# One phase for the output projection and the MLP, with the second norm's factor applied after w_up

## The chip, the core and the metric

The kernel runs on one core of one Trainium2 chip. The metric is the device time of one execution in microseconds (us). The core's engines run side by side and meet only at semaphores: PE multiplies matrices (its weight loads are shown as PEld), ACT and DVE work element by element and can read the matmul banks, POOL works element by element on on-chip memory, and SP issues the DMAs.

## What is computed

One layer of a hybrid decoder, for 1,040 prompt tokens (16 of them learned meta tokens) and 8 sequences of 4 sampled tokens. The part that matters here is what follows the attention and the convolution:

```python
mix = jnp.concatenate([_rmsnorm(attn, attn_out_g), _rmsnorm(conv, conv_out_g)], axis=-1)
x = x + mix @ w_o                          # 1024 x 1024
hf = _rmsnorm(x, norm_ffn_g)               # x * rsqrt(mean(x*x) + EPS) * gain
return x + jnp.square(jax.nn.relu(hf @ w_up)) @ w_down      # 1024 x 4096, 4096 x 1024
```

## The kernel before

Six phases follow one another: `inputs`, `prompt_attention`, `sample_attention`, `output_projection`, `mlp` and `store_outputs`. Each ends with a barrier of all engines (L321). Activations are kept transposed: features on the 128 partitions, 1,074 columns of tokens in 3 blocks of 358 (`NBLK`, `TB`), so that the residual stream `xT` has 8 chunks of 128 features (`KD`).

Weight products come close to float32 by splitting: a number is kept as a rounded part `hi` and a remainder `lo`, and each product takes three matmul passes, hi by hi, hi by lo and lo by hi. A weight tile of 128 output columns goes through a `Ring` of two slots: SP loads `raw`, ACT rounds it to `hi` (`split_hi`, L229), POOL subtracts (`split_lo`, L233). `split_hi` waits until the slot's last product is done (`used`), SP's next load until `split_lo` is done (`lo_done`). `Ring.products` (L236, matmuls at L244) then issues for each chunk k the three passes over three blocks, 72 matmuls for a `KD`-chunk tile, into three banks of slot 0 or of slot 1, and waits before that until those banks have been emptied (`evacuated`).

`Norm` (L97) is an RMS norm over features. ACT and DVE square the chunks, POOL adds pairs, PE sums over partitions by matmuls with ones (L152), DVE takes the mean (L158), ACT the root (L165), DVE the reciprocal (L161), PE spreads the factor over the partitions (L171) and ACT copies it out of the banks (L176). Only then does DVE scale chunk by chunk (L181), ACT round `hi` (L191), and DVE and POOL in turn subtract `lo` (L196, L201).

`output_projection` (L1808) runs two such norms over 4 chunks each, then 8 tiles of `w_o`. The first two are issued interleaved as the normed chunks come (`paired_products`, L249, matmuls at L266), the other six in a loop; after each, DVE adds the banks into its chunk of `xT` (L1894). After the barrier `mlp` (L1897) starts with the norm over all 8 chunks of `xT` and pairs the first two `w_up` tiles. It then works in 8 groups of 4 tiles of `w_up` (f = 0 to 3) and 8 tiles of `w_down` (m = 0 to 7, 4 chunks each). After a `w_up` product ACT applies the relu from the banks (L1949) and squares into `a_hi` (L1953), DVE squares again (L2035) and subtracts (`a_lo`, L2038). The first `w_down` product takes chunk k only when `a_lo` of f = k is done (`act_ready`). DVE adds each `w_down` product into `xT` (L2045).

## Time and profile before

| | us |
|---|---|
| three runs | 2112.9, 2110.64, 2107.7; median 2110.64 |
| the profiled execution, whole | 2108.73 |
| its span, first to last instruction | 2107.0 |
| PE busy in the span | 2002.8 (95%) |
| DVE, ACT, POOL busy | 928.2, 796.6, 428.4 |

In the span the output projection begins at 1179 us, the MLP at 1302 us and the store of the outputs at 2088 us. All starts below are counted from the span's first instruction. "Granted clock" (PEclk) is the share of full TensorE speed that the chip allowed: 1.00 is 2.4 GHz, 0.50 is 1.2 GHz, and a value between the two is a mean over a stretch with both. A row's idle time stands in square brackets or behind a bar, with what ended it.

### The profile page before, as it was taken

How to read it: one execution, taken by the hardware profiler on the slowest of the kernel's cores; microseconds unless marked ns; L12 is line 12 of the kernel's file. 1: busy time of each engine (PE TensorE's matmuls, PEld its weight loads, DVE VectorE, ACT ScalarE, POOL GpSimd, SP SyncE). 2: the span in 40 equal slices, each digit the busy share in tenths (PEclk: the TensorE clock that was granted, in tenths of full speed). 3: DMA queues.
4: the chain of work that ended last, by engine and by line, in shares of the span. 5: the costliest groups of instructions: out<-in, count | busy, mean ns of one | idle time of the engine just before them, and what ended most of it. 6: DMA issues, size and time to landing. Idle time of an engine off the chain costs nothing. (4 is left out here: it accounts for less than half of the span.)

```text
span 2107.0 us, 38039 instructions
## 1 busy us (share of the span) xinstructions
PE 2002.8 (95%) x13358; PEld 1877.5 (89%) x13358; DVE 928.2 (44%) x1679; ACT 796.6 (38%) x1702; POOL 428.4 (20%) x391
## 2 busy tenths in 40 slices
PE   6999997999969999999999698899999999999998
PEld 5999985777749999999998496799999999999998
DVE  6125145556536777777777622521222222221222
ACT  5012134656635666666666311311121111212121
POOL 3233133111010000010000323331222222231221
PEclk7999998999979999999999598899999999999999
DMA  6122000000022222222222111020202011120202
GB/s 213 50 64 63 10 19 9 1 1 0 0 71 63 77 74 73 70 75 73 74 69 107 40 40 29 22 61 26 75 15 65 25 55 50 30 61 24 75 15 97
DMA packets 180599, 108.42 MB, mean 51 GB/s; under 512 B 52132, under 2 KB 177154, under 8 KB 180276
## 3 DMA queue, kind: packets, MB, share of 16 engines
q1 hardware_dynamic: 180358, 107.21, 17.7%
q8 instruction: 44, 0.72, 0.1%
q10 hardware_dynamic: 174, 0.30, 0.1%
q14 instruction: 23, 0.19, 0.0%
HBM read 97.47 MB, written 10.00 MB: 51 GB/s over the span
## 5 line engine op out<-in xcount | busy, mean ns | idle before, releaser
L1750 PE MATMUL banks<-comb_hi,pageT_hi 128*128 128x272 f32 x1024 | 234.3, 310 | 0.0
L1640 DVE TENSOR_REDUCE k_sums<-k_sq 128x8 f32<-128x512 f32 x256 | 174.4, 681 | 92.3 <-ACT k_sq L1462 92.3
L1750 PE MATMUL banks<-comb_hi,pageT_lo 128*128 128x272 f32 x1024 | 212.5, 289 | 0.0
L1750 PE MATMUL banks<-comb_lo,pageT_hi 128*128 128x272 f32 x1024 | 212.2, 289 | 0.0
L1462 ACT ACTIVATE k_sq<-banks 128x512 f32<-128x512 f32 x256 | 152.0, 594 | 142.4 <-PE banks L1750 139.4
L2045 DVE TENSOR_TENSOR xT<-xT,banks 128x1074 f32<-128x1074 f32 x64 | 81.5, 1274 | 277.4 <-PE banks L244 277.4
L2035 DVE TENSOR_TENSOR relu_squared<-relu 128x1074 f32<-128x1074 f32 x32 | 40.9, 1278 | 305.2 <-ACT relu L1949 305.2
L1949 ACT ACTIVATE relu<-banks 128x1074 f32<-128x1074 f32 x32 | 34.3, 1071 | 360.3 <-PE banks L244 351.9
L244 PE MATMUL banks<-a_hi,w_down_hi 128*128 128x358 f32 x768 | 168.2, 327 | 0.0
L244 PE MATMUL banks<-a_hi,w_down_lo 128*128 128x358 f32 x768 | 167.7, 326 | 0.0
L244 PE MATMUL banks<-a_lo,w_down_hi 128*128 128x358 f32 x768 | 167.6, 326 | 0.0
L233 POOL TENSOR_TENSOR w_down_lo<-w_down_raw,w_down_hi 128x512 fp32r<-128x512 f32 x64 | 94.7, 1479 | 348.0 <-ACT w_down_hi L229 348.0
L1750 PEld LDWEIGHTS banks<-comb_lo,pageT_hi 128*128 128x128 f32 x1024 | 161.8, 189 | 0.0
L1750 PEld LDWEIGHTS banks<-comb_hi,pageT_lo 128*128 128x128 f32 x1024 | 161.0, 190 | 0.0
L1750 PEld LDWEIGHTS banks<-comb_hi,pageT_hi 128*128 128x128 f32 x1024 | 158.1, 191 | 0.0
L244 PE MATMUL banks<-hf_hi,w_up_lo 128*128 128x358 f32 x720 | 157.5, 327 | 0.0
L244 PE MATMUL banks<-hf_hi,w_up_hi 128*128 128x358 f32 x720 | 157.0, 326 | 0.3 <-POOL w_up_lo L233 0.3
L244 PE MATMUL banks<-hf_lo,w_up_hi 128*128 128x358 f32 x720 | 157.1, 326 | 0.0
L244 PEld LDWEIGHTS banks<-a_hi,w_down_hi 128*128 128x128 f32 x768 | 133.3, 189 | 0.0
L244 PEld LDWEIGHTS banks<-a_hi,w_down_lo 128*128 128x128 f32 x768 | 132.8, 189 | 0.0
L244 PEld LDWEIGHTS banks<-a_lo,w_down_hi 128*128 128x128 f32 x768 | 131.6, 189 | 0.0
L229 ACT CAST w_down_hi<-w_down_raw 128x512 fp32r<-128x512 f32 x64 | 39.5, 617 | 237.4 <-PE banks L244 237.4
(371 smaller groups left out, 4044.3 us busy)
## 6 DMA issues: line engine op xcount, KB each, us to landing
page_latents<-in_cache_kv_latent SPq DMA_DIRECT2D x256, 128.0 KB, 2.1
w_up_raw<-in_w_up SPq DMA_DIRECT2D x32, 512.0 KB, 4.2
w_down_raw<-in_w_down SPq DMA_DIRECT2D x64, 256.0 KB, 2.8
w_in_raw<-in_w_in SPq DMA_DIRECT2D x17, 512.0 KB, 3.8
x_spill<-xT SPq DMA_DIRECT2D x1, 4296.0 KB, 13.9
xT<-x_spill SPq DMA_DIRECT2D x1, 4296.0 KB, 12.8
page_ropes<-in_cache_k_rope SPq DMA_DIRECT2D x256, 16.0 KB, 1.8
w_o_raw<-in_w_o SPq DMA_DIRECT2D x8, 512.0 KB, 4.2
```

Source lines behind the costliest of these rows:

```text
L229: act.copy(self.hi[s][:, :, :], self.raw[s][:, :, :]).then_inc(self.hi_done[s], 1)
L233: nc.gpsimd.tensor_sub(self.lo[s][:, :, :], self.raw[s][:, :, :], self.hi[s][:, :, :].bitcast(F32)).then_inc(self.lo_done[s], 1)
L244: mm = pe.matmul(out[:, b, 0:TB], w[s][:, k, :], x(k)[:, b * TB:(b + 1) * TB], start=k == 0 and a == 0, stop=k == self.K - 1 and a == 2)
L1462: act.activation(sq[j % 2][:, :].rearrange("p (a c) -> p a c", a=2), kn[:, :, 0:WK], ACT.Square)\
L1640: nc.vector.tensor_reduce(ksum[par][:, j, :], sq[j % 2][:, :].rearrange("p (h c) -> p h c", h=H), AX_X, ALU.add)\
L1750: mm = pe.matmul(banks[:, 2 * (j % 2) + half, 0:WC], x[j % AHEAD][:, k, :], w[par][:, k, half, :], start=k == 0 and a == 0, stop=k == KL - ...
L1949: act.activation(relu[:, f % 2, :].rearrange("p (b t) -> p b t", b=NBLK), banks[:, 3 * (f % 2):3 * (f % 2) + 3, 0:TB], ACT.Relu)\
L2035: nc.vector.tensor_mul(full[:, s, :], relu[:, s, :], relu[:, s, :]).then_inc(sq_done, 1)
L2045: nc.vector.tensor_add(x, x, banks[:, 3 * s:3 * s + 3, 0:TB]).then_inc(down.evacuated[s], 1)
```

## The change

The two phases become one, `output_and_mlp`, and the norm before the MLP is taken apart in a new class `LateNorm`. Its per-token factor is a positive number, so it can be taken out of `hf @ w_up` and through the relu: the products are made from `x * gain`, and the factor is multiplied in when the results of `w_up` leave the banks.

- `w_o` and `w_up` share one ring and its two slots of banks; SP loads `w_up` tiles behind the `w_o` tiles. The loop over `w_o` tiles 2 to 7 is written out on every engine. `w_down` keeps its ring, now in memory that held the convolution's and the attention's results, so its first loads wait for the last `w_o` product.
- As soon as DVE has added tile m into `xT`, ACT rounds `x * gain` of that chunk and squares the chunk, DVE subtracts the remainder, POOL adds the square to a running total.
- PE sums the total over partitions inside the first `w_up` product (f = 0, before chunk 6), in a bank of its own, and spreads the factor inside the second (f = 1, before chunk 2); its third spread waits for ACT's copy of the first. The first two `w_up` tiles are no longer interleaved.
- In the MLP, DVE empties the banks of each `w_up` product with one instruction, max(bank, 0) times the factor, in place of ACT's relu. The squares and the subtraction stay as they are, with the DVE square written where `a_lo` goes.
- The two norms ahead of `w_o` write their scaled chunks in place and keep their squares elsewhere; their steps stay the same.

```diff
-        for phase in (inputs, prompt_attention, sample_attention, output_projection, mlp, store_outputs):
+        for phase in (inputs, prompt_attention, sample_attention, output_and_mlp, store_outputs):
...
-def output_projection(g):
...
+class LateNorm:
...
+        self.sums = g.banks[:, low_bank, :]
+        self.spread_bank = [g.banks[:, b, :] for b in (high_bank, low_bank, high_bank)]
...
+    def act_hi(self, act, c):
+        act.activation(self.hi(c), self.src(c), ACT.Copy, scale=self.gain(c)).then_inc(self.hi_done, 1)
+    def act_square(self, act, c):
+        if c > 1:
+            act.wait_ge(self.added, c - 1)
+        act.activation(self.total if c == 0 else self.square, self.src(c), ACT.Square).then_inc(self.squared, 1)
+    def pool_add(self, pool, c):
+        pool.wait_ge(self.squared, c + 1)
+        if c > 1:
+            pool.wait_ge(self.added, c - 1)
+        self.nc.gpsimd.tensor_add(self.total, self.total, self.square).then_inc(self.added, 1)
+    def dve_lo(self, v, c):
+        v.wait_ge(self.hi_done, c + 1)
+        self.nc.vector.scalar_tensor_tensor(self.lo(c), self.src(c), self.gain(c), self.hi(c).bitcast(F32),
+                                            ALU.mult, ALU.subtract).then_inc(self.lo_done, 1)
+    def pe_sums(self, pe):
+        pe.wait_ge(self.added, self.K - 1)
+        for b in range(NBLK):
+            mm = pe.matmul(self.sums[b * self.Q:(b + 1) * self.Q, 0:TB], self.g.ones[:, 0:self.Q],
+                           self.total[:, b * TB:(b + 1) * TB], start=True, stop=True)
+        mm.then_inc(self.summed, 1)
+    def dve_inverse(self, v):
+        v.wait_ge(self.summed, 1)
+        self.nc.vector.tensor_scalar(self.roots, self.sums[0:NBLK * self.Q, 0:TB], 1.0 / self.width, EPS,
+                                     ALU.mult, ALU.add).then_inc(self.mean, 1)
+        v.wait_ge(self.root, 1)
+        self.nc.vector.reciprocal(self.roots, self.roots).then_inc(self.root_inv, 1)
+    def act_root(self, act):
+        act.wait_ge(self.mean, 1)
+        act.activation(self.roots, self.roots, ACT.Sqrt).then_inc(self.root, 1)
+    def pe_spread(self, pe):
+        pe.wait_ge(self.root_inv, 1)
+        for b in range(NBLK):
+            row = slice(b * self.Q, b * self.Q + 1)
+            if b == 2:
+                pe.wait_ge(self.inv_done, 1)
+            pe.matmul(self.spread_bank[b][:, 0:TB], self.g.ones[row, :], self.roots[row, :], start=True, stop=True)\
+                .then_inc(self.spread, 1)
+    def act_inverse(self, act):
+        for b in range(NBLK):
+            act.wait_ge(self.spread, b + 1)
+            act.copy(self.inv[:, b * TB:(b + 1) * TB], self.spread_bank[b][:, 0:TB]).then_inc(self.inv_done, 1)
...
+def output_and_mlp(g):
...
+    ring = Ring(sem, "w_out_up", ar, KD)
...
+    a_lo, a_full = low.take_twice("a_lo", [P, FC, TT])
...
+    norm = LateNorm(g, "ffnnorm", ffn_scratch, lambda c: xT[:, c, :], KD, D, lambda c: g.gcol[:, G_FFN + c:G_FFN + c + 1],
+                    lambda c: hf_hi[:, c, :], lambda c: hf_lo[:, c, :], square[:, :], total[:, :], 6, 7)
...
+    turn = lambda i, f: KD // 2 + i * (FC // 2) + f // 2
...
+            for m in range(KD):
+                sp.wait_ge(ring.lo_done[m % 2], m // 2 + 1)
+                sp.dma_start(ring.raw[m % 2][:, :, :], w_o[:, :, m * P:(m + 1) * P]).then_inc(ring.loaded[m % 2], 16)
+            with sp.Fori(0, GROUPS) as i:
+                for f in range(FC):
...
+                    if m < 2:
+                        sp.wait_ge(ring.used[1], KD // 2 + 1)
...
-            with act.Fori(1, KD // 2) as i:
-                for s in range(2):
-                    ring.split_hi(act, s, i)
+            for m in range(KD):
+                ring.split_hi(act, m % 2, (m + 2) // 2)
+                act.wait_ge(ring.evacuated[m % 2], m // 2 + 2)
+                norm.act_hi(act, m)
+                norm.act_square(act, m)
+            norm.act_root(act)
+            norm.act_inverse(act)
+            def group(i, first):
+                if not first:
+                    ring.split_hi(act, 0, turn(i, 0))
+                for f in range(FC):
+                    if f == 0 and first:
+                        pass
+                    elif f + 1 < FC:
+                        ring.split_hi(act, (f + 1) % 2, turn(i, f + 1))
+                    else:
+                        down.split_hi(act, 0, i * per)
+                    act.wait_ge(ring.evacuated[f % 2], turn(i, f) + 2)
+                    act.activation(a_hi[:, f, :], relu[:, f % 2, :], ACT.Square).then_inc(hi_done, 1)
+                for m in range(1, KD):
+                    down.split_hi(act, m % 2, i * per + m // 2)
...
-            with pool.Fori(1, KD // 2) as i:
-                for s in range(2):
-                    ring.split_lo(nc, pool, s, i)
+            for m in range(KD):
+                ring.split_lo(nc, pool, m % 2, (m + 2) // 2)
+                if m > 0:
+                    norm.pool_add(pool, m)
...
+            for m in range(2, KD):
+                pe.wait_ge(ring.evacuated[m % 2], m // 2 + 1)
+                ring.products(pe, m % 2, m // 2, slot(m % 2), lambda k: mix_hi[:, k, :], mix_lo)
+            def group(i, first):
+                for f in range(FC):
+                    s = f % 2
+                    def ready(k, f=f):
+                        if f == 0:
+                            pe.wait_ge(norm.lo_done, k + 1)
+                            if k == 6:
+                                norm.pe_sums(pe)
+                        elif f == 1 and k == 2:
+                            norm.pe_spread(pe)
+                    if first and f < 2:
+                        pe.wait_ge(ring.evacuated[s], KD // 2 + 1)
+                    elif f < 2:
+                        pe.wait_ge(down.evacuated[s], i * per + 1)
+                    else:
+                        pe.wait_ge(ring.evacuated[s], turn(i, f) + 1)
+                    ring.products(pe, s, turn(i, f), slot(s), lambda k: hf_hi[:, k, :], lambda k: hf_lo[:, k, :],
+                                  first=ready if first and f < 2 else None)
...
+                            pe.wait_ge(act_ready, i * FC + (k + 1))
...
-def mlp(g):
...
-                    act.wait_ge(up.used[f % 2], i * 2 + (f // 2 + 2))
-                    act.wait_ge(act_ready, i * FC + max(f, 1))
-                    act.activation(relu[:, f % 2, :].rearrange("p (b t) -> p b t", b=NBLK),
-                                   banks[:, 3 * (f % 2):3 * (f % 2) + 3, 0:TB], ACT.Relu)\
-                        .then_inc(up.evacuated[f % 2], 1)
-                    act.wait_ge(up.evacuated[f % 2], i * 2 + (f // 2 + 1))
-                    act.activation(a_hi[:, f, :], relu[:, f % 2, :], ACT.Square).then_inc(hi_done, 1)
...
-                    paired_products(pe, up, lambda s: banks[:, 3 * s:3 * s + 3, :], range(KD), lambda k: hf_hi[:, k, :],
-                                    lambda k: hf_lo[:, k, :], lambda k: norm.wait_lo(pe, k))
...
-                    v.wait_ge(up.evacuated[s], i * 2 + (f // 2 + 1))
-                    v.wait_ge(act_ready, i * FC + max(f, 1))
-                    nc.vector.tensor_mul(full[:, s, :], relu[:, s, :], relu[:, s, :]).then_inc(sq_done, 1)
...
-                    nc.vector.tensor_sub(a_lo[:, f, :], full[:, s, :], a_hi[:, f, :].bitcast(F32))\
...
+            for m in range(KD):
+                v.wait_ge(ring.used[m % 2], m // 2 + 2)
+                x = blocked(xT[:, m, :])
+                nc.vector.tensor_add(x, x, slot(m % 2)[:, :, 0:TB]).then_inc(ring.evacuated[m % 2], 1)
+                norm.dve_lo(v, m)
             norm.dve_inverse(v)
-            norm.dve_scale(v)
+            v.wait_ge(norm.inv_done, NBLK)
+            inv = blocked(norm.inv[:, :])
             with v.Fori(0, GROUPS) as i:
                 for f in range(FC):
                     s = f % 2
-                    v.wait_ge(up.evacuated[s], i * 2 + (f // 2 + 1))
-                    v.wait_ge(act_ready, i * FC + max(f, 1))
-                    nc.vector.tensor_mul(full[:, s, :], relu[:, s, :], relu[:, s, :]).then_inc(sq_done, 1)
+                    v.wait_ge(ring.used[s], turn(i, f) + 2)
+                    nc.vector.scalar_tensor_tensor(blocked(relu[:, s, :]), slot(s)[:, :, 0:TB], 0.0, inv, ALU.max, ALU.mult)\
+                        .then_inc(ring.evacuated[s], 1)
+                    v.wait_ge(ring.evacuated[s], turn(i, f) + 2)
+                    nc.vector.tensor_mul(a_full[:, f, :], relu[:, s, :], relu[:, s, :]).then_inc(sq_done, 1)
...
```

## Rows read from the trace of the kernel before

**Rows 1.** Busy us by stretch: length, PE, PEld, DVE, ACT, POOL, PEclk, DMA, GB/s.
```profile
1228.10:1299.50 71.40, 71.40 (x434) 71.11 (x432) 7.64 (x6) 5.27 (x5) 12.00 (x5) 1.00 0.09 28
1299.50:1325.40 25.90, 9.19 (x43) 1.86 (x43) 17.47 (x11) 9.88 (x10) 12.15 (x5) 0.62 0.38 102
1325.40:1354.70 29.30, 27.48 (x145) 26.47 (x145) 20.17 (x11) 9.94 (x10) 15.94 (x5) 0.87 0.00 1
1354.70:2088.50 733.80, 733.80 (x4464) 733.75 (x4464) 159.50 (x125) 132.54 (x155) 169.18 (x93) 1.00 0.15 42
```

**Rows 2.** Timeline of PE around the gap: start, duration, engine, line, instruction.
```profile
1298.85 0.66 PE L244 MATMUL banks<-mix_hi,w_o_lo 128*128 128x358 f32 x3
...
1308.15 1.42 PE L152 MATMUL banks<-hf_lo_before,ones 128*32 128x358 f32 x6 [2.04 <-DVE hf_lo_before L136]
...
1319.00 1.36 PE L171 MATMUL banks<-ffn_norm_roots,ones 1*128 1x358 f32 x6 [3.60 <-DVE ffn_norm_roots L161]
...
1354.70 0.72 PE L244 MATMUL banks<-hf_hi,w_up_hi 128*128 128x358 f32 x3 [0.31 <-POOL w_up_lo L233]
```

**Rows 3.** Timeline of DVE: the adds after w_o tiles 6 and 7.
```profile
1287.82 1.27 DVE L1894 TENSOR_TENSOR xT<-xT,banks 128x1074 f32 x1 [10.58 <-PE banks L244]
1299.66 1.27 DVE L1894 TENSOR_TENSOR xT<-xT,banks 128x1074 f32 x1 [10.57 <-PE banks L244]
```

**Rows 4.** Timeline of the gap: the factor's chain on DVE and ACT.
```profile
1315.46 0.53 DVE L158 TENSOR_SCALAR ffn_norm_roots<-banks 96x358 f32<-96x358 f32 x1 [3.91 <-PE banks L152]
1316.02 0.50 ACT L165 ACTIVATE ffn_norm_roots<-ffn_norm_roots 96x358 f32<-96x358 f32 x1 [6.87 <-DVE ffn_norm_roots L158]
1316.56 2.39 DVE L161 RECIPROCAL ffn_norm_roots<-ffn_norm_roots 96x358 f32<-96x358 f32 x1 [0.57 <-ACT ffn_norm_roots L165]
...
1320.41 1.05 ACT L176 COPY ffn_norm_inv<-banks 128x1074 f32<-128x1074 f32 x1 [3.88 <-PE banks L171]
```

**Rows 5.** Groups by line and shape: times, mean ns, idle before.
```profile
L644 ACT ACTIVATE conv_y<-conv_u,gain_columns 128x1040 f32<-128x1040 f32 x4 | 5.0, 1257 | 0.0
L229 ACT CAST w_up_hi<-w_up_raw 128x1024 fp32r<-128x1024 f32 x32 | 32.6, 1041 | 1.1 <-DMA w_up_raw<-in_w_up 1.1
L1106 ACT COPY probsT<-banks 128x384 f32<-128x384 f32 x16 | 7.6, 472 | 3.0 <-PE banks L1228 3.0
```

**Rows 6.** Single lines and tiles: duration ns min/median/max, first and last start.
```profile
L201 POOL TENSOR_TENSOR hf_lo<-hf_lo_before,hf_hi x4: 2504/3572/3592, 1325.3 to 1343.0; 128x1074 fp32r<-128x1074 f32 x4
L233 POOL TENSOR_TENSOR w_up_lo<-w_up_raw,w_up_hi x32: 2337/2726/3380, 1310.4 to 2021.0; 128x1024 fp32r<-128x1024 f32 x32
L181 DVE SCALAR_TENSOR_TENSOR hf_lo_before<-xT,gain_columns,ffn_norm_inv x8: 1324/1334/3579, 1321.5 to 1338.2; 128x1074 f32<-128x1074 f32 x8
L789 DVE SCALAR_TENSOR_TENSOR cq_lo<-banks,gain_columns,cq_hi x3: 1334/1335/1336, 197.0 to 223.0; 128x1074 fp32r<-128x1074 f32 x3
L2045 DVE TENSOR_TENSOR xT<-xT,banks x64: 1273/1274/1275, 1384.5 to 2088.8; 128x1074 f32<-128x1074 f32 x64
```

**Rows 7.** Timeline of the last group: from w_up tile 3 into w_down tile 0.
```profile
2040.74 0.65 PE L244 MATMUL banks<-hf_hi,w_up_lo 128*128 128x358 f32 x3
...
2041.51 1.07 ACT L1949 ACTIVATE relu<-banks 128x1074 f32<-128x1074 f32 x1 [9.12 <-PE banks L244]
...
2042.62 1.10 ACT L1953 ACTIVATE a_hi<-relu 128x1074 fp32r<-128x1074 f32 x1
2042.62 1.28 DVE L2035 TENSOR_TENSOR relu_squared<-relu 128x1074 f32<-128x1074 f32 x1 [9.24 <-ACT relu L1949]
...
2043.93 1.28 DVE L2038 TENSOR_TENSOR a_lo<-relu_squared,a_hi 128x1074 fp32r<-128x1074 f32 x1
...
2045.51 0.52 PEld L244 LDWEIGHTS banks<-a_hi,w_down_hi 128*128 128x128 f32 x3
```

**Rows 8.** Busy time by short stretch, as PE starts again after the gap.
```profile
1330.00:1332.00 2.00, 2.00 (x8) 2.00 (x8) 2.00 (x2) 1.09 (x1) 0.82 (x1) 0.50 0.00 0
1334.00:1336.00 2.00, 1.10 (x7) 1.13 (x8) 2.00 (x2) 0.08 (x1) 0.75 (x1) 1.00 0.00 0
```

More of the change, by code:

```diff
@@ L1825, in output_projection @@
+    hi_done, sq_done, act_ready = sem("a_hi_done"), sem("a_squared"), sem("a_ready")
+    w_o = A["w_o"].rearrange("(k p) n -> p k n", p=P)
+    w_up = A["w_up"].rearrange("(k p) n -> p k n", p=P)
+    w_down = A["w_down"].rearrange("(g k p) n -> p g k n", k=FC, p=P)
+    per = KD // 2
+    turn = lambda i, f: KD // 2 + i * (FC // 2) + f // 2
     with nc.Block() as block:
@@ L1852, in _ @@
             ring.open(pool, ring.lo_done)
+            down.open(pool, down.lo_done)
             conv.pool_pairs(pool)
@@ L2014, in hidden @@
                         if m == 0:
-                            pe.wait_ge(act_ready, i * FC + (k + 2))
-                    down.products(pe, s, i * per + m // 2, banks[:, 3 * s:3 * s + 3, :],
+                            pe.wait_ge(act_ready, i * FC + (k + 1))
+                    down.products(pe, s, i * per + m // 2, slot(s),
                                   lambda k: a_hi[:, k, :], lambda k: a_lo[:, k, :], first=hidden)
```

196 lines of the change are left out of this document (71 added, 125 removed).

## The prediction

> **What bounds the kernel now.** I first read busy time by stretch [rows 1]. In the last six `w_o` products and in the MLP from its third `w_up` tile on, PE is busy all the time, 71.40 of 71.40 us and 733.80 of 733.80 us, at a granted clock of 1.00: there nothing but fewer matmuls would help. Between them lie 25.90 us in which PE does little (its 9.19 us are sums and spreads for the norm) and 29.30 us in which it starts on `w_up`, part of it at 1.2 GHz (mean clock 0.87). The change works on these two stretches and leaves the matmul passes of the weights as they are.
>
> Then the timeline of PE [rows 2]. The last `w_o` pass ends at 1298.85 + 0.66 = 1299.51 us; I call this moment E. The third `w_up` tile begins at 1354.70, so **E to the third tile takes 55.19 us**. In it PE has two tiles to do. What a tile costs at full clock is seen in DVE's adds: tiles 6 and 7 of `w_o` are added 1299.66 - 1287.82 = 11.84 us apart [rows 3]; I take 11.85. Two tiles are 23.7 us, so 31.5 us of the 55.19 are gap and slow start.
>
> The gap is a chain in which every member is waited for: squares, sums, mean, root, reciprocal, spread, copy [rows 4], then scale and split.
>
> **The change, part by part: what PE now finds after E.** PE begins f = 0 at once if its weights and its first chunks are there. The weights are loaded and split behind tile 6, one product (11.85 us) earlier, as every tile's are now. Chunks 0 to 6 are rounded and squared while later `w_o` products run: per chunk DVE has an add and a subtraction, ACT three passes of 1.0 to 1.3 us, POOL two of 2.4 to 3.6 us [rows 3, 5, 6], all well within 11.85 us. Of chunk 7 this is left, counted from E: the add takes 1.27 and is done at 1.4 (it begins 0.15 after E, [rows 2, 3]); ACT has rounded the next weights (1.04) meanwhile. Rounding with a gain column I take from the nearest form, 1.26, done at 2.7, the square as 1.1, done at 3.85 [rows 5, 7]. POOL splits the weights of f = 1 from about 1.2 on and needs 2.4 to 3.4, then adds the square in 2.5 to 3.6: 6.4 to 8.2 [rows 6]. PE wants the total before chunk 6, 6/8 of 11.85 = 8.9 after E. **No wait there, with 0.7 to 2.5 us to spare.** DVE's remainder of chunk 7 takes 1.33, or 3.58 beside POOL [rows 6]: done by 6.3, wanted after 10. So the norm's squares, and its eight scale and split steps, cost nothing on the path; PE covers them. The new waits: ACT waits for each add, and behind that stands the rounding of the next weights but one, which is wanted a product later; POOL waits for each square, and behind that stands the split of the same weights, again a product early. If that cover were gone, one chunk's steps would cost what chunk 7's do, 6.4 to 8.2 us.
>
> What PE gains in instructions: one set of sums and the spreads. A set of sums for one chunk (6 records) took 1.42 us, three spreads 1.36 us, both in a stretch at half clock [rows 2]. Here PE has not been idle, so I expect full clock and half of each, 0.7 and 0.7; the rows themselves are the upper ends, 1.4 and 1.4. The third spread waits for ACT's copy of the first: a copy of 384 columns from a bank is 0.47 us [rows 5], the second spread covers some 0.25 of that and two hand-overs of about 0.1 come on top: 0.4, between 0 and 0.7.
>
> Is the factor late? Sums end at 8.9 + 0.7 = 9.6. Mean 0.53, root 0.50 and reciprocal 2.39 with hand-overs are 1318.95 - 1315.46 = 3.5 us [rows 4], so 13.2 with one more hand-over. PE reaches chunk 2 of f = 1 at 11.85 + 0.7 + 2.96 = 15.5: no wait, 2.3 us to spare. The spreads and copies end near 17.3. DVE, which waits with f = 0 in its banks until then, empties them in 1.34 (18.7), ACT squares (1.10) and only behind this, in its own order, rounds the weights of f = 2 (1.04): 20.9; POOL splits them in 2.73, at most 3.38: 23.6 to 24.3 [rows 5 to 7]. PE wants them when f = 1 ends, at 23.7 + 0.7 + 0.7 + 0.4 = **25.5 us after E**. So this queue behind the factor is the tightest of the three, 1.2 to 1.9 us, but holds.
>
> E to the third tile: 25.5 us in place of 55.19. **Gain 29.7 us**; 27.2 (28.0 gained) with the upper ends of sums, spreads and copy, 24.4 (30.8 gained) with the lower.
>
> **The MLP's groups.** Work moves from ACT to DVE: ACT's relu from the banks takes 1.07 us; DVE's instruction of the same kind with one operand in a bank and one in memory takes 1.335 [rows 6, 7]. It matters in one place per group: the first `w_down` product wants chunk 3 a little after f = 3 ends. With F = 2040.74 + 0.65 = 2041.39, relu starts at F + 0.12, the remainder is done at F + 3.82, and PE loads chunk 3's weights at F + 4.12 [rows 7]: 0.30 spare. Now 0.12 + 1.335 + 1.28 + 1.28 and two hand-overs of 0.04 give F + 4.1. A release has to travel too, so I put 0.05 us of PE wait on each group, 0.4 us in eight; from 0 to 8 x 0.26 = 2.1 us.
>
> The Trainium skill ("VectorE: DVE Perf Modes", Specifications) speaks against this move: it places VectorE closer to SBUF and ScalarE closer to PSUM. The rows agree in direction (1.07 against 1.335). If all of the difference reached PE, 8 x 0.265 = 2.1 us would be lost, which is the upper end above; by the spare time, most of it is not.
>
> What ACT loses (32 relus) and the barrier fewer free nothing on the path in the MLP, where PE is full. SP's loads of `w_up` now stand behind those of `w_o`, and `w_down`'s first loads wait for E; they are wanted some 49 us later, after four tiles. The two norms before `w_o` keep their steps: nothing for them. The written-out `w_o` loop I price at nothing too: the first MLP group was written out before and lies in the 733.80 us in which PE is never idle [rows 1].
>
> **Sum.** 29.7 - 0.4 = 29.3 us. The profiled execution's 2108.73 us (span 2107.0) becomes 2079.4. The median of the runs is 2110.64, 1.9 above it; on that basis **2081.3 us**. The bounds of the unknown costs alone (gain 25.9 to 30.8) give 2079.8 to 2084.7; the three runs before lie up to 2.9 us from their median, which makes 2077 to 2088.
>
> **Rivals.** (1) *The queue behind the factor is late.* f = 2's weights come after PE wants them, or the total after chunk 6. Against it speak 1.2 and 0.7 us of spare time; for it, that POOL's and DVE's instructions grow from 2.5 to 3.6 and from 1.33 to 3.58 us beside each other [rows 6] and may all do so in one chain. Two such growths beyond the spare time cost about 3 us: 2084.
>
> (2) *The gate of each group moves to DVE.* If the new instruction grows to 3.58 us in all groups, remainders come 2.2 us later than PE wants them: 8 x 2.2 = 17.6 us lost, 2099. Against it: DVE's 64 adds with one operand in a bank lie between 1.273 and 1.275 us, never longer [rows 6]. A smaller loss per group, 0.3 to 0.5, gives 2083 to 2086.
>
> (3) *Slower than before: each group's wait also drops the clock.* After the gap PE came back at 0.50 and, though busy, was still there between 1330 and 1332 us [rows 8]; the time at half clock, from the start of `w_up` at 1325.4 to after 1332, is 7 us, so 3.5 lost. If rival 2's wait brought this on in every group, 8 x (2.2 + 3.5) = 45.6 us would go: 2110.64 - 29.7 + 45.6 = 2126.5. It decides from 29.7 / 8 = 3.7 us per group on. Against it: between 1334 and 1336 PE was busy for 1.10 of 2 us and the clock stayed at 1.00 [rows 8], so a wait of under 1 us did not bring the clock down; the waits would have to be long first. The Trainium skill describes such a case ("TensorE: Matmul & The Clock Gate", HAM oscillation), where a wait in each tile lets the clock fall each time; the long gap here fits it (clock 0.62 over 25.9 us, [rows 1]), the short one does not.
>
> (4) *It doesn't do what it says*: the factor's chain still stands between `w_o` and `w_up`, only elsewhere. Then the 31.5 us stay: 2110. By the order of waits PE needs no factor before it has issued 1.25 tiles, which speaks against it.
>
> **How the numbers follow.** Forecast 0.72; rival 1 0.12; rival 2, mostly in its small form, 0.12; rivals 3 and 4 0.02 each. The range takes in the forecast's own spread, rival 1 and the small form of rival 2, and ends at 2077 and 2089; about 0.15 to 0.2 is left out. A measurement of this kernel can tell about 0.3% (6.3 us) from no change. Faster by more than that: all but rivals 3 and 4, 0.96; within it, rival 4, 0.02; slower, rival 3, 0.02.
>
> **What would show it.** In the new trace PE should have no idle time of over 1 us from tile 2 of `w_o` to the end of the MLP, a granted clock of 1.00 throughout, and about 25.5 us between the last `w_o` pass and the third `w_up` tile. Sums and spreads should show PE waiting at most for ACT's copy. If PE waits before f = 2 for POOL, rival 1 holds; if it waits at chunk 3 of each first `w_down` product for DVE, rival 2; a clock under 1.00 in the groups is rival 3. The forecast falls if the two phases before `w_o`'s loop get longer, which I have not priced, or if the mean tile in the MLP departs from 11.85 us.

## Result and the profile after

| | before | after |
|---|---|---|
| median (lowest to highest of four runs), us | 2110.03 (2107.7 to 2112.9) | 2085.43 (2082.69 to 2087.84) |
| profiled execution, whole; span | 2108.73; 2107.0 | 2082.69; 2080.9 |
| PE busy in the span | 2002.8 (95%) | 1993.6 (96%) |

The changed kernel takes 0.9879 of the time before (95% interval 0.9863 to 0.9896). It is 24.6 us faster by the medians and 26.0 by the profiled executions, where 29.3 was forecast.

First the busy time by stretch (length, PE, PEld, DVE, ACT, POOL, granted clock, DMA, GB/s), against [rows 1]:

```profile
1228.00:1298.70 70.70, 70.70 (x431) 70.70 (x431) 20.47 (x12) 19.18 (x18) 35.45 (x12) 1.00 0.17 48
1298.70:1313.00 14.30, 14.30 (x90) 13.49 (x89) 6.37 (x4) 3.74 (x4) 5.91 (x2) 1.00 0.26 73
1313.00:1316.60 3.60, 3.06 (x16) 1.76 (x14) 0.00 (x0) 0.82 (x2) 0.00 (x0) 1.00 0.00 0
1316.60:1318.60 2.00, 2.00 (x9) 2.00 (x9) 1.23 (x1) 0.46 (x1) 0.00 (x0) 0.62 0.03 8
1318.60:1320.60 2.00, 2.00 (x9) 2.00 (x8) 1.93 (x3) 1.91 (x2) 0.00 (x0) 0.52 0.01 4
1320.60:1327.00 6.40, 6.40 (x41) 6.40 (x40) 0.68 (x1) 0.12 (x1) 2.72 (x1) 1.00 0.00 0
1327.10:2062.60 735.50, 735.48 (x4466) 735.18 (x4464) 199.04 (x156) 99.60 (x124) 168.65 (x93) 1.00 0.15 42
```

The gap is gone: PE is busy through E, now at 1298.70, and on. What is left stands in rows three to five: 0.54 us without work, and then 4 us in which PE is busy all the time at a mean clock of 0.62 and 0.52, so about 3.4 us of them at half clock.

The timeline of PE shows the same stretch pass by pass (start, duration, engine, line, instruction; in brackets idle time and what ended it). It stands against [rows 2]:

```profile
1298.05 0.65 PE L244 MATMUL banks<-mix_hi,w_out_up_lo 128*128 128x358 f32 x3
1298.54 0.66 PE L244 MATMUL banks<-hf_hi,w_out_up_hi 128*128 128x358 f32 x3
...
1306.93 0.65 PE L244 MATMUL banks<-hf_hi,w_out_up_lo 128*128 128x358 f32 x3
1307.51 0.80 PE L1852 MATMUL banks<-ffn_total,ones 128*32 128x358 f32 x6
1308.24 0.76 PE L244 MATMUL banks<-hf_hi,w_out_up_hi 128*128 128x358 f32 x3
...
1313.79 0.65 PE L244 MATMUL banks<-hf_hi,w_out_up_lo 128*128 128x358 f32 x3
1314.36 0.87 PE L1873 MATMUL banks<-ffn_norm_roots,ones 1*128 1x358 f32 x4
1315.78 0.86 PE L1873 MATMUL banks<-ffn_norm_roots,ones 1*128 1x358 f32 x2 [0.54 <-ACT ffn_norm_inv L1879]
1316.57 0.86 PE L244 MATMUL banks<-hf_hi,w_out_up_hi 128*128 128x358 f32 x3
...
1320.68 0.65 PE L244 MATMUL banks<-hf_hi,w_out_up_lo 128*128 128x358 f32 x3
...
1327.11 0.66 PE L244 MATMUL banks<-hf_hi,w_out_up_hi 128*128 128x358 f32 x3
```

The last `w_o` pass ends at 1298.05 + 0.65, and f = 0 has begun in its shadow. A pass of three blocks starts every 0.494 us at full clock (11.867 us a tile, by 24). The sums push the next pass from 1306.93 + 0.494 to 1308.24: 0.82 us. The spread pushes its next pass from 1313.79 + 0.494 = 1314.28 to 1316.57: 2.29. From there five passes take until 1320.68, 4.11 us where 2.47 were due: 1.64 lost to half clock. 23.7 + 0.82 + 2.29 + 1.64 = 28.45, and 1327.11 - 1298.70 = 28.41 was measured.

The **ledger** of the two spans:

| part | before | after | difference |
|---|---|---|---|
| span start to E | 1299.51 | 1298.70 | -0.81 |
| E to the third `w_up` tile | 55.19 | 28.41 | -26.78 |
| third tile to the last add | 734.09 | 735.50 | +1.41 |
| last add to the span's end | 18.21 | 18.29 | +0.08 |

The first line can't be read as work of the change: PE does the same products there, and the point E varies by several us from one profile of the changed kernel to the next, as the table below shows.

### The profile page after: what moved, and what is told of

Its sections match the earlier page's. It is cut to its first block and busy times, and to the rows that moved or that the text cites. A ratio compares the mean times of both kernels' runs of the same rounds, so it can differ in the third digit from the quotient of the medians.

```text
span 2080.9 us, 37740 instructions
## 1 busy us (share of the span) xinstructions
PE 1993.6 (96%) x13328; PEld 1875.8 (90%) x13328; DVE 955.6 (46%) x1703; ACT 767.5 (37%) x1676; POOL 432.2 (21%) x392
## 5 line engine op out<-in xcount | busy, mean ns | idle before, releaser
L1989 ACT ACTIVATE a_hi<-relu 128x1074 fp32r<-128x1074 f32 x32 | 35.4, 1105 | 396.0 <-DVE relu L2095 396.0
L244 PE MATMUL banks<-hf_hi,w_out_up_hi 128*128 128x358 f32 x768 | 169.3, 329 | 0.0
L244 PE MATMUL banks<-hf_hi,w_out_up_lo 128*128 128x358 f32 x768 | 168.4, 327 | 0.0
L244 PE MATMUL banks<-hf_lo,w_out_up_hi 128*128 128x358 f32 x768 | 168.4, 327 | 0.0
L2095 DVE SCALAR_TENSOR_TENSOR relu<-banks,ffn_norm_inv 128x1074 f32<-128x1074 f32 x32 | 40.8, 1276 | 268.9 <-PE banks L244 263.4
L233 POOL TENSOR_TENSOR w_out_up_lo<-w_out_up_raw,w_out_up_hi 128x1024 fp32r<-128x1024 f32 x40 | 101.7, 2551 | 272.2 <-ACT w_out_up_hi L229 272.2
L244 PEld LDWEIGHTS banks<-hf_hi,w_out_up_hi 128*128 128x128 f32 x768 | 133.2, 190 | 1.1 <-issue 1.1
L244 PEld LDWEIGHTS banks<-hf_lo,w_out_up_hi 128*128 128x128 f32 x768 | 133.1, 190 | 0.0
L244 PEld LDWEIGHTS banks<-hf_hi,w_out_up_lo 128*128 128x128 f32 x768 | 133.1, 189 | 0.0
```

The lines of the kernel that those rows point to most:

```text
L233: nc.gpsimd.tensor_sub(self.lo[s][:, :, :], self.raw[s][:, :, :], self.hi[s][:, :, :].bitcast(F32)).then_inc(self.lo_done[s], 1)
L244: mm = pe.matmul(out[:, b, 0:TB], w[s][:, k, :], x(k)[:, b * TB:(b + 1) * TB], start=k == 0 and a == 0, stop=k == self.K - 1 and a == 2)
L1989: act.activation(a_hi[:, f, :], relu[:, f % 2, :], ACT.Square).then_inc(hi_done, 1)
L2095: nc.vector.scalar_tensor_tensor(blocked(relu[:, s, :]), slot(s)[:, :, 0:TB], 0.0, inv, ALU.max, ALU.mult)\
```

## Experiments

Unless a diff says otherwise, an edit starts from the changed kernel. Whole times differ between profiles by several us because of what comes before E, so stages are compared too, all read from DVE's adds: "S" from the add of `w_o` tile 7 to the first add of `w_down`, "MLP" from that to the last of the 64.

| kernel | add of `w_o` tile 7 | S | MLP | median | ratio to before (95%) |
|---|---|---|---|---|---|
| before | 1299.66 | 84.8 | 704.3 | 2110.03 | |
| after | 1298.74 | 58.3 | 705.6 | 2085.43 | 0.9879 (0.9863 to 0.9896) |
| after_again | 1299.36 | 58.2 | 705.6 | 2083.70 | 0.9884 (0.9867 to 0.9900) |
| e1_third_spread_later | 1299.30 | 57.4 | 705.7 | 2084.77 | 0.9887 (0.9870 to 0.9903) |
| e2_factor_first | 1300.86 | 72.2 | 705.7 | 2098.78 | 0.9953 (0.9937 to 0.9970) |
| e3_relu_on_act | 1300.85 | 58.2 | 705.6 | 2084.18 | 0.9881 (0.9864 to 0.9899) |
| e5_weights_early | 1301.27 | 56.3 | 705.6 | 2082.95 | 0.9875 (0.9859 to 0.9892) |
| e6_ring_below | 1299.97 | 58.3 | 707.4 | 2087.16 | 0.9899 (0.9883 to 0.9916) |
| e8_split_late | 1300.73 | 67.6 | 705.6 | 2094.11 | 0.9930 (0.9914 to 0.9947) |
| e11_lo_moved | 1302.40 | 56.3 | 706.3 | 2083.50 | 0.9876 (0.9860 to 0.9893) |
| e10_more_small | 1298.18 | 59.0 | 705.6 | 2081.74, one run | |
| e4_two_waits | 1305.10 | 61.1 | 705.6 | 2092.09, one run | |

The second column moves between 1298.2 and 1305.1 without an edit to what lies before it. S and MLP repeat to 0.1 us in the two profiles of the unaltered kernel. Two more kernels, e7 and e9, have waits added inside the MLP and are told in the text.

### Where the gain comes from

**e2_factor_first: the factor finished ahead of the first product.**

```diff
-                            if k == 6:
+                            if k == 0:
                                 norm.pe_sums(pe)
-                        elif f == 1 and k == 2:
-                            norm.pe_spread(pe)
+                                norm.pe_spread(pe)
+                                pe.wait_ge(norm.inv_done, NBLK)
+                            pe.wait_ge(norm.lo_done, k + 1)
```

> Sums and spreads are issued ahead of the first w_up product, which waits for the whole factor: the chain stands between w_o and w_up again, but the chunks' scale and split stay beside the w_o products. By the forecast's steps: total 7 to 8 us after the last w_o pass, sums 0.8, mean to reciprocal 3.5, spreads and copies 3: PE idle for about 13 us more than now, and 3.5 us of half clock when it starts again, against the 1.7 us that it pays today: 14 to 16 us slower than the changed kernel, so about 2098 to 2101. The rest of the gain, 9 to 12 us, then belongs to the early split of the chunks and the barrier. Rival (the late factor hides little, since most of the old gap was the eight chunks): less than 6 us slower.

Measured: S grew from 58.3 to 72.2 us and the median to 2098.78, 13 to 15 us over the unaltered kernel. PE's timeline shows the factor's chain as waits (E is 1300.17 + 0.65):

```profile
1300.17 0.65 PE L244 MATMUL banks<-mix_hi,w_out_up_lo 128*128 128x358 f32 x3
1307.97 1.41 PE L1852 MATMUL banks<-ffn_total,ones 128*32 128x358 f32 x6 [7.15 <-POOL ffn_total L1842]
1312.96 1.56 PE L1873 MATMUL banks<-ffn_norm_roots,ones 1*128 1x358 f32 x4 [3.58 <-DVE ffn_norm_roots L1861]
1315.07 1.56 PE L1873 MATMUL banks<-ffn_norm_roots,ones 1*128 1x358 f32 x2 [0.54 <-ACT ffn_norm_inv L1879]
```

That is the chain the prediction took off the path: 7.15 us until the total is there (add, square, POOL's split of the next weights, POOL's add), 3.58 for mean, root and reciprocal, then the spread, at half clock. Putting the factor first gives back some 14 of the 26.5 us by which S had shrunk.

**e8_split_late: the chunks rounded and split only when all `w_o` products are done.**

```diff
             for m in range(KD):
                 ring.split_hi(act, m % 2, (m + 2) // 2)
                 act.wait_ge(ring.evacuated[m % 2], m // 2 + 2)
-                norm.act_hi(act, m)
                 norm.act_square(act, m)
+            for m in range(KD):
+                norm.act_hi(act, m)
...
+            for m in range(KD):
                 norm.dve_lo(v, m)
```

> ACT squares each finished chunk at once as in the changed kernel, but rounds all eight, and DVE subtracts, only after the last w_o product; the factor still comes late. By the forecast's rows: first remainder 5 to 7 us after the last w_o pass, PE idle until then, half clock when it starts (3.5 us lost), chunks at 1.2 to 2.2 us beside 1.5 of PE: 8 to 10 us slower than the changed kernel, about 2092 to 2095. With e2_factor_first (15 us slower) that would make up nearly the whole gain of 26 us. Rival (PE covers the splits, since they keep pace with it): under 4 us slower.

Measured: S 67.6, 9.3 us more; median 2094.11. One row of PE's timeline tells it; the clock was 0.51 from 1308 to 1312.

```profile
1307.95 0.94 PE L244 MATMUL banks<-hf_hi,w_out_up_hi 128*128 128x358 f32 x2 [7.26 <-DVE hf_lo L1846]
```

So the gain has two parts that can be told apart: some 14 us from the factor's late use, some 9 from the early split. Either alone leaves a wait of over 7 us. Together they are 23 of the 26.5 us; no run took both away, so whether the rest is the barrier between the phases or an overlap of the two is not shown.

**e3_relu_on_act: ACT empties the banks again.** The factor is made but left out of the product, so this kernel computes something else; it serves for times alone.

```diff
+                    act.wait_ge(ring.used[f % 2], turn(i, f) + 2)
...
+                    act.activation(blocked(relu[:, f % 2, :]), slot(f % 2)[:, :, 0:TB], ACT.Relu)\
+                        .then_inc(ring.evacuated[f % 2], 1)
...
-                    nc.vector.scalar_tensor_tensor(blocked(relu[:, s, :]), slot(s)[:, :, 0:TB], 0.0, inv, ALU.max, ALU.mult)\
-                        .then_inc(ring.evacuated[s], 1)
```

> ACT applies the relu from the banks as in the kernel before, and DVE no longer empties them; the norm's factor is made but left out of the product, so this kernel computes the MLP without it. It shows what DVE's emptying costs in the groups. Forecast: 0 to 2.1 us over eight groups, mostly hidden. If the slower pace of the MLP (94.87 us per group against 94.69) comes from DVE reading the banks beside PE, the groups return to 94.69 and about 1.4 us go. Rival (the pace differs from execution to execution): it stays where the unaltered kernel of this series lies. DVE need not wait for the factor here, so f = 2's weights come earlier, which should bring nothing, as PE does not wait for them now.

Measured: S 58.2, MLP 705.6, median 2084.18: nothing changes. The move of the relu to DVE costs nothing, and the MLP's 1.3 us over the kernel before do not come from DVE emptying the banks.

### What the spread costs

**after_again: the changed kernel as it is**, for whether the half clock behind the spread is of the kernel or of one execution.

> The changed kernel unaltered, once more, as the yardstick of this series. Theory A (what the forecast lacks lies in the spread: 2.2 us of PE time in place of 1.1, and 3.4 us at half clock behind it): again about 2083 to 2087 us, with a granted clock near 0.5 for 3 to 4 us behind the spread, and 28 to 29 us from the last w_o pass to the third w_up tile. Theory B (the clock falls by chance of the moment): the half-clock stretch is missing or of quite another length. On the MLP's pace (94.87 us per group against 94.69 before): if it belongs to the change, it is again 94.8 or more; if it is the spread between executions, it moves by as much as 0.1 to 0.2 us.

Measured: 2083.70, and the same fall. Busy time by stretch:

```profile
1317.00:1319.00 2.00, 2.00 (x8) 1.81 (x8) 1.01 (x1) 0.46 (x1) 0.00 (x0) 0.65 0.03 8
1319.00:1321.00 2.00, 2.00 (x9) 2.00 (x8) 1.93 (x3) 1.70 (x2) 0.00 (x0) 0.50 0.02 4
```

In all five profiles with the spread as it is (after, after_again, e3, e6, e8) the clock falls behind it.

**e1_third_spread_later: the third spread two chunks on, ahead of chunk 4**, where ACT's copy is long done.

```diff
-    def pe_spread(self, pe):
+    def pe_spread(self, pe, blocks=range(NBLK)):
...
-        for b in range(NBLK):
+        for b in blocks:
...
-                            norm.pe_spread(pe)
+                            norm.pe_spread(pe, range(2))
+                        elif f == 1 and k == 4:
+                            norm.pe_spread(pe, range(2, 3))
```

> The third spread is issued before chunk 4 of f = 1 in place of right behind the second, so PE no longer waits for ACT's copy. Theory A: PE's wait of 0.5 to 1.1 us goes and with it the fall of the clock: 2 to 3 us less than the unaltered kernel, clock 1.00 throughout, about 25.8 us from the last w_o pass to the third w_up tile. Rival A2 (the small matmuls of sums and spreads bring the clock down, not the idle time): only the wait's 0.5 to 1 us goes, and there is still a stretch near 0.5 behind them. Rival B: nothing but the wait changes, and a fall comes elsewhere.

Measured: the wait is gone and the clock stays up, but S falls by only 0.9 us, to 57.4. Stretches, and the third `w_up` tile in PE's timeline:

```profile
1316.00:1322.00 6.00, 6.00 (x34) 5.26 (x34) 1.48 (x2) 1.30 (x4) 0.00 (x0) 1.00 0.02 3
...
1326.78 0.73 PE L244 MATMUL banks<-hf_hi,w_out_up_hi 128*128 128x358 f32 x3 [0.89 <-POOL w_out_up_lo L233]
```

2 to 3 us less were expected. With the last third of the factor later, the queue behind it (DVE's emptying, ACT's square and rounding, POOL's subtraction) is later too. POOL's split shows it:

```profile
1323.92 2.71 POOL L233 TENSOR_TENSOR w_out_up_lo<-w_out_up_raw,w_out_up_hi 128x1024 fp32r<-128x1024 f32 x1 [17.53 <-ACT w_out_up_hi L229]
```

It ends at 1326.63, 27.4 us after E (1298.61 + 0.65 here), against 24.8 in the changed kernel. PE, which is faster by what the wait and the half clock took, now waits for it: the mechanism of the prediction's rival 1, at 0.89 us.

**e5_weights_early: the same, and ACT rounds the weights of f = 2 ahead of the factor's copies.**

```diff
             norm.act_root(act)
+            ring.split_hi(act, 0, turn(0, 2))
             norm.act_inverse(act)
...
-                    if f == 0 and first:
+                    if f < 2 and first:
```

> The third spread is issued before chunk 4 as in e1_third_spread_later, and ACT rounds the weights of f = 2 right after the root, before it copies the factor, in place of behind the square of f = 0. In e1 PE waited 0.9 us for POOL's split of those weights. Theory (the fall of the clock came from the wait in the spread, and e1's gain was eaten by the queue behind the factor, rival 1 of the prediction): clock 1.00 throughout, no wait ahead of f = 2, 26.3 us from the last w_o pass to the third w_up tile against 28.4: about 2 us less than the unaltered kernel, 2081 to 2083. Rival: something else is late before f = 2 (the factor for f = 0's banks), and the stretch stays near 27.5.

Measured: S 56.3, 1.9 us less than unaltered; E to the third tile is 1327.70 - 1301.23 = 26.5. PE waits for nothing between 1299 and 1335, and around the spreads the stretch shows

```profile
1317.00:1323.00 6.00, 6.00 (x32) 4.76 (x33) 0.54 (x1) 1.27 (x3) 0.61 (x1) 1.00 0.01 3
```

Here the forecast's 25.5 us are missed by only 1.0. There is neither wait nor half clock, and what PE's passes are pushed back by is 0.82 us at the sums, 0.89 at the first two spreads and 0.90 at the third alone. POOL splits f = 2's weights at 1315.23, some ten us ahead of need. No version has a shorter S; it takes 2082.95 us in all, and its whole time can't be told from that of the unaltered kernel (the intervals overlap), the stage can.

### What brings the clock down

Two explanations stood: PE's wait of 0.54 us, or the spread's matmuls themselves, whose operand has one row (1x358).

**e10_more_small: e5 with the first two spreads issued three times, no wait.**

```diff
+        for b in (0, 1, 0, 1) if len(blocks) == 2 else ():
+            row = slice(b * self.Q, b * self.Q + 1)
+            pe.matmul(self.spread_bank[b][:, 0:TB], self.g.ones[row, :], self.roots[row, :], start=True, stop=True)
         for b in blocks:
```

> e5_weights_early with four more one-row spread matmuls into the same two banks ahead of the first two spreads, and no wait: six one-row matmuls in a row, some 2.3 to 2.6 us. Theory C1 (one-row matmuls count little for the clock): the clock falls behind them for 3 to 4 us although PE never waits. Rival C2 (they must come together with a wait): the clock stays at 1.00 and only their own time of about 1.6 us is added.

Measured (timeline of PE, and two stretches behind the spreads):

```profile
1313.80 1.47 PE L1871 MATMUL banks<-ffn_norm_roots,ones 1*128 1x358 f32 x8
1315.11 0.77 PE L1876 MATMUL banks<-ffn_norm_roots,ones 1*128 1x358 f32 x4
1315.81 0.84 PE L244 MATMUL banks<-hf_hi,w_out_up_hi 128*128 128x358 f32 x3
1316.45 1.10 PE L244 MATMUL banks<-hf_lo,w_out_up_hi 128*128 128x358 f32 x3
...
1316.00:1318.00 2.00, 2.00 (x9) 2.00 (x9) 0.00 (x0) 0.72 (x2) 0.00 (x0) 0.59 0.04 8
1318.00:1320.00 2.00, 2.00 (x9) 2.00 (x8) 0.00 (x0) 0.00 (x0) 0.00 (x0) 0.56 0.00 0
```

The clock falls although PE is never idle: behind six one-row matmuls in 2.0 us, it needs no wait. The five passes from 1315.81 on take until 1319.92, 4.11 us, as in the changed kernel. In e5, with two of them (0.87 us), six full passes, and one more (0.86 us), it stayed at 1.00. Chance of the moment is an unlikely rival: in all five profiles with the third spread apart and no added small matmuls (e1, e5, e7, e9, e11) the clock stayed at 1.00 around the spreads. No run had three one-row matmuls in a row without a wait, so how much of the changed kernel's fall is due to the wait and how much to the matmuls is not shown.

**e4_two_waits: all three spreads through one bank, so two waits.**

```diff
-        self.spread_bank = [g.banks[:, b, :] for b in (high_bank, low_bank, high_bank)]
+        self.spread_bank = [g.banks[:, b, :] for b in (high_bank, high_bank, high_bank)]
...
-            if b == 2:
-                pe.wait_ge(self.inv_done, 1)
+            if b > 0:
+                pe.wait_ge(self.inv_done, b)
```

> The changed kernel with all three spreads in one bank, so that the second and the third each wait for ACT's copy: the spread takes some 3.4 us in place of 2.2. The clock should fall again behind it, as in all profiles of the changed kernel, with 3.4 us or more at half. Theory C: the whole is 1 to 2 us slower than the unaltered kernel, as the wait is added but the fall is the same. Rival (each wait brings its own share of the fall): the half-clock stretch grows to 5 us or more.

Measured: S 61.1, 2.8 us more than with one wait. PE's timeline and three of the stretches:

```profile
1322.13 0.86 PE L1873 MATMUL banks<-ffn_norm_roots,ones 1*128 1x358 f32 x2 [0.55 <-ACT ffn_norm_inv L1879]
1323.55 1.56 PE L1873 MATMUL banks<-ffn_norm_roots,ones 1*128 1x358 f32 x2 [0.55 <-ACT ffn_norm_inv L1879]
...
1322.00:1324.00 2.00, 1.32 (x3) 0.75 (x4) 0.00 (x0) 0.54 (x2) 0.00 (x0) 0.83 0.00 0
1324.00:1326.00 2.00, 2.00 (x5) 1.01 (x5) 0.16 (x1) 0.46 (x1) 0.00 (x0) 0.50 0.03 8
...
1330.00:1332.00 2.00, 2.00 (x13) 2.00 (x13) 0.00 (x0) 0.00 (x0) 1.99 (x1) 0.96 0.00 0
```

The clock falls already ahead of the third spread (1.56 us, not 0.86) and stays at 0.50 until just after 1330: 6.8 us at half clock in place of about 3.4. The theory that the fall would be the same is wrong, and the expectation's rival holds: the length of the fall is not fixed, and the longer thin stretch cost more.

**e7_idle and e9_longer_idle: e5 with waits of PE alone in the first MLP group, ahead of `w_down` tiles 2, 4 and 6**, for copies that ACT makes on memory that nobody uses then.

```diff
+                        if fresh and k == 0 and m in (2, 4, 6):
+                            pe.wait_ge(pong, (1, 2, 4)[m // 2 - 1])
...
+                        for n in ((1,) if m == 3 else (2,) if m == 5 else (3, 4)):
...
+                            act.copy(square[:, 0:wide], total[:, 0:wide]).then_inc(pong, 1)
```

e9 takes 2, 2 and 3 whole copies in place of a short one, 1 and 2.

> e5_weights_early with three added waits of PE in the first group, each for a copy that ACT starts when the product before ends: before w_down tile 2 some 0.75 us, before tile 4 some 1.25 us, before tile 6 some 2.4 us, with full matmuls right up to each and no small ones. Theory (idle time of about 1 us is enough): the clock falls behind the second and third, and stays at half for 3 to 4 us each time. Rival (idle time alone must be longer; in the spread it was the small matmuls with the wait): it falls behind the third only, or behind none.

> As e7_idle, where pure waits of 0.80, 1.27 and 2.39 us between full matmuls left the clock at 1.00, which was against the theory that the wait alone brought it down. Here the three waits are 2.4, 2.4 and 3.5 us. Theory C (idle time alone is harmless up to here, and the spread needs its one-row matmuls as well): no fall behind the first two, perhaps one behind the third. Rival (e7's longest wait met a lucky moment): a fall behind at least one of the two of 2.4 us.

Measured in e7: waits of 0.80, 1.27 and 2.39 us, and a clock of 1.00 in all stretches behind them. That speaks against the theory that a wait of 0.54 us brings the clock down by itself, and so does e1, where the clock stayed at 1.00 behind a wait of 0.89 us; each length was seen once. In e9 (PE's timeline, then the stretch behind each wait):

```profile
1363.73 0.40 PE L244 MATMUL banks<-a_hi,w_down_hi 128*128 128x358 f32 x1 [2.39 <-ACT ffn_square L1999]
1379.74 0.40 PE L244 MATMUL banks<-a_hi,w_down_hi 128*128 128x358 f32 x1 [2.39 <-ACT ffn_square L1999]
1395.35 0.40 PE L244 MATMUL banks<-a_hi,w_down_hi 128*128 128x358 f32 x1 [3.51 <-ACT ffn_square L1999]
...
1365.00:1368.00 3.00, 3.00 (x12) 3.00 (x12) 0.00 (x0) 0.00 (x0) 0.47 (x1) 0.54 0.27 81
1380.00:1383.00 3.00, 3.00 (x20) 3.00 (x20) 0.00 (x0) 0.11 (x1) 1.30 (x1) 1.00 0.08 23
1395.00:1398.00 3.00, 2.65 (x11) 2.68 (x12) 0.00 (x0) 2.63 (x4) 2.20 (x2) 0.66 0.00 0
```

Two waits of the same 2.39 us: the clock fell behind one and not behind the other, nor behind e7's; it fell behind the one of 3.51 us. e9's theory, no fall behind the first two, is wrong. What decides between equal waits stays open. The two kernels were run once each, 2088.49 (e7) and 2093.32 us (e9).

### The pace of the MLP

**e6_ring_below: the new ring, the total and the square placed below the normed chunks.** Only addresses change.

```diff
+    ring = Ring(sem, "w_out_up", ar, KD)
+    total, square = (ar.take(n, [P, TT], F32) for n in ("ffn_total", "ffn_square"))
...
-    ring = Ring(sem, "w_out_up", ar, KD)
-    total, square = (ar.take(n, [P, TT], F32) for n in ("ffn_total", "ffn_square"))
```

> Only addresses change: the ring of w_o and w_up and the two tiles of the running total lie below the normed chunks in memory in place of above. The MLP's adds from first to last took 704.3 us before and 705.6 to 705.7 in every form of the changed kernel so far, with ACT's relu too. If the place of the operands in memory makes the 1.3 us, the adds' stretch changes here by more than 0.2 us. If it is the order of work, it stays at 705.6.

**e11_lo_moved: e5 with total and square ahead of the remainders `hf_lo`**, which move up by 8.6 KB a partition.

```diff
+    total, square = (ar.take(n, [P, TT], F32) for n in ("ffn_total", "ffn_square"))
     hf_lo = ar.take("hf_lo", [P, KD, TT], F32R)
     ring = Ring(sem, "w_out_up", ar, KD)
-    total, square = (ar.take(n, [P, TT], F32) for n in ("ffn_total", "ffn_square"))
```

> e5_weights_early with the running total's two tiles placed ahead of hf_lo, so that hf_lo lies 8.6 KB higher in each partition and the ring stays where it is. The MLP's adds took 705.6 us in seven profiles with the ring above and 707.4 with all of ring and total moved below. If hf_lo's own address matters, this one changes by over 0.2 us; if only the ring's does, it stays at 705.6. The whole should lie within 2 us of e5_weights_early.

Measured, as DVE's adds in the MLP (ns least, median, most; first and last start): of the kernel after, then e6, then e11; [rows 6] has the line of before.

```profile
L2107 DVE TENSOR_TENSOR xT<-xT,banks x64: 1273/1273/1276, 1357.0 to 2062.6; 128x1074 f32<-128x1074 f32 x64
...
L2107 DVE TENSOR_TENSOR xT<-xT,banks x64: 1273/1274/1276, 1358.3 to 2065.7; 128x1074 f32<-128x1074 f32 x64
...
L2110 DVE TENSOR_TENSOR xT<-xT,banks x64: 1273/1274/1276, 1358.7 to 2065.0; 128x1074 f32<-128x1074 f32 x64
```

The same matmuls in the same order take 705.6, 707.4 and 706.3 us, by addresses alone; before it was 704.3. In the nine profiles that keep the addresses and add nothing inside the MLP it is 705.6 or 705.7. Most of it lies in the products of `w_up`, whose operands moved: by the starts of DVE's emptying a `w_up` tile takes 11.87, 11.93 and 11.89 us in the three, a `w_down` tile 5.93 in all. That the 1.3 us between before and after are of this kind is likely (their size is that of e6's step, and e3 excludes DVE's emptying of the banks), but not shown: no run had the new order at the old addresses. Which operand matters, and how, stays open.

## Why the prediction was right, and where not

**The gap and its chain: right.** The chain left the path, 26.8 of 55.2 us of the stretch went, and e2 and e8 put back about 14 and 9 us of it. The result lies inside the range; the gain forecast was 3 to 5 us too large.

**The sums behind the range.** The prediction's lower end for E to the third tile, 24.4 us (gain 30.8), does not follow from its terms: with 0.7, 0.7 and no wait for the copy the sum is 25.1 (gain 30.1). So the fast end of its unknown costs, 2079.8, should have been 2080.5; the slow end, on whose side the result lies, is not touched.

**Chunk 7 and the total: right.** Timelines of DVE and POOL behind E (1298.70):

```profile
1298.74 1.27 DVE L2086 TENSOR_TENSOR xT<-xT,banks 128x1074 f32<-128x1074 f32 x1 [7.12 <-PE banks L244]
...
1301.28 2.19 DVE L1846 SCALAR_TENSOR_TENSOR hf_lo<-xT,gain_columns,hf_hi 128x1074 fp32r<-128x1074 f32 x1 [1.26 <-ACT hf_hi L1831]
1302.31 3.52 POOL L1842 TENSOR_TENSOR ffn_total<-ffn_total,ffn_square 128x1074 f32<-128x1074 f32 x1
```

The total is done at 1305.83, 7.1 us after E (6.4 to 8.2 forecast), and PE's sums find it there. POOL's add (3.52) and DVE's subtraction (2.19) both grew beside each other, as [rows 6] let expect: in e8, where seven of the eight subtractions run with no add beside them, those take 1.33. The spare time took it. The sums cost 0.82 (0.7 forecast): full clock, right.

**The spread: the step that failed.** "Here PE has not been idle, so I expect full clock and half of each, 0.7 and 0.7", and 0.4 for the wait: 1.1 us in all. Measured 2.29, and behind it 1.64 more at half clock: 3.9. Two things were missed. The 1.36 us of [rows 2] were taken for half clock throughout; the busy time of that stretch of the kernel before, read at finer steps, says otherwise:

```profile
1318.90:1320.40 1.50, 1.36 (x6) 0.31 (x6) 0.04 (x1) 0.00 (x0) 0.00 (x0) 0.62 1.08 322
```

At a clock of 0.62, 1.36 us are not to be halved. And one spread costs as much as two in a row: in e5 two push the passes back by 0.89 us, one alone by 0.90. With its third matmul behind a wait, the spread pays for two groups and the wait: 0.96 from 1314.28 to the end of the first two, 0.54 of waiting, and 0.79 from the third's start to the next pass, 2.29. Secondly, "a wait of under 1 us did not bring the clock down", read from [rows 8], held for plain waits as far as they were tried (e7's 0.80 us and e1's 0.89 didn't either) but says nothing of one-row matmuls: behind six of them the clock fell without any wait (e10). "A granted clock of 1.00 throughout" was wrong at this one place, with 3.4 us at half clock. The term of the sum is the stretch's 25.5, which measured 28.4; with the spreads apart (e5) it measures 26.5.

In the MLP's groups the granted clock was 1.00 from 1327.10 to 2062.60: what the Trainium skill calls HAM oscillation ("TensorE: Matmul & The Clock Gate"), a clock that falls again at the wait of each tile, did not occur there. The same page, under "A second HAM failure mode: psum-queue depth-cycling", tells of a clock that falls where the engine is idle shortly but often between groups of matmuls. The spread's wait is such a short idle time, but a single one; and e10 differs from the page's case, as there the clock fell (0.59, 0.56) with no idle time at all.

**The queue behind the factor: right, though half a microsecond late.** f = 2's weights were done 24.8 us after E (23.6 to 24.3 forecast), still ahead of the forecast's 25.5, and PE wanted them only at 28.4:

```profile
1317.38 1.28 DVE L2095 SCALAR_TENSOR_TENSOR relu<-banks,ffn_norm_inv 128x1074 f32<-128x1074 f32 x1 [5.52 <-ACT ffn_norm_inv L1879]
...
1320.80 2.72 POOL L233 TENSOR_TENSOR w_out_up_lo<-w_out_up_raw,w_out_up_hi 128x1024 fp32r<-128x1024 f32 x1 [14.97 <-ACT w_out_up_hi L229]
```

So 0.7 us would have been left even at the forecast pace. It had been called the tightest of the three, rightly: e1 gave back the time of the wait and the half clock but made this queue 2.6 us later, and PE waited 0.89 us for it.

**The MLP's gate: wrong size, wrong cause.** 0.4 us of waits at chunk 3 were forecast from 1.335 us for DVE's emptying. It took less, and no group waits. All 32, and the last group (there F = 2014.51 + 0.65 = 2015.16), against [rows 7]:

```profile
L2095 DVE SCALAR_TENSOR_TENSOR relu<-banks,ffn_norm_inv x32: 1275/1276/1277, 1317.4 to 2015.2; 128x1074 f32<-128x1074 f32 x32
...
2015.20 1.27 DVE L2095 SCALAR_TENSOR_TENSOR relu<-banks,ffn_norm_inv 128x1074 f32<-128x1074 f32 x1 [7.96 <-PE banks L244]
2017.83 1.28 DVE L2101 TENSOR_TENSOR a_lo<-a_lo_before,a_hi 128x1074 fp32r<-128x1074 f32 x1
2019.29 0.35 PEld L244 LDWEIGHTS banks<-a_hi,w_down_hi 128*128 128x128 f32 x2
```

The remainder is done at F + 3.95 and loaded at F + 4.13, on time. The row chosen for the price, L789 of [rows 6], multiplies by a column; this one has a constant there and takes about as long as the adds, 1.27. The column is the likely reason, since L181 of [rows 6], with a column and no bank, takes 1.334 too; but the rows differ in their operations as well. That the Trainium skill ("VectorE: DVE Perf Modes", Specifications) places ScalarE closer to PSUM, where the matmul banks are, agrees with 1.07 against 1.28 here. Since PE waited for none of these steps, giving the relu back to ACT changed nothing (e3). What the MLP did lose, 1.3 to 1.4 us, is pace: a `w_up` tile takes 11.867 us after and 11.83 before. No step of the prediction priced addresses; it named "if the mean tile in the MLP departs from 11.85 us" among what would make it fall.

**Rivals.** Rival 1 did not occur in the changed kernel; its mechanism showed when the factor came later (e1). Rival 2 did not (705.6 us with ACT's relu as with DVE's). Rival 3's mechanism, a fall of the clock by a thin stretch, came once and not per group. Rival 4 did not occur: PE is busy through E.

**From the profile to the medians.** 26.78 - 1.41 = 25.4 us are of the change by the stages; 29.3 - 25.4 = 3.9 us is the error, of which the spread has 2.9 and the pace 1.0. The medians give 24.6; the rest lies in what varies before E.

## What to carry to other kernels

A positive factor per token can be applied behind the product, and chunks can be split as they are finished: the norm's whole chain then hides behind two products. But price what stands behind the factor in each engine's queue, since it is late next. Where the small matmuls go matters as much as when their data is there: put one or two of them at a time between full passes and give the copy that frees a bank a few passes, rather than have all of them in one place with a wait. Compare such kernels by stages between fixed instructions: here those repeated to 0.1 us, while whole executions moved by several.

## What the runs showed of the hardware

- The clock fell to 1.2 GHz with PE busy all the time, behind six one-row matmuls in 2.0 us (e10), which lost 4.11 - 2.47 = 1.64 us; behind waits of 0.80 and 1.27 us among full products it did not (e7), behind 2.39 us it did once in three times, and behind 3.51 us it did (e7, e9).
- Addresses of operands in on-chip memory alone moved the pace of the same fp32 products by 0.1 to 0.3%: the MLP took 705.6 us after, 706.3 with the remainders `hf_lo` and the two tiles of the total moved (e11), 707.4 with the ring below the chunks (e6).
- DVE's product with an operand in a bank took 1.276 us with a constant (L2095) and 1.335 with a column as its scalar (L789), for 1,074 columns; the two differ in their operations too.
